# A layer of two blocks on one core: six row slots for the down rows and ten for the up rows behind the first 160 gathers, instead of sixteen for both

## The chip, the cores and the metric

The kernel runs on one core of a Trainium2 chip. Its time is the device time of one execution, in microseconds; lower is better. The engines are TensorE (PE; PEld is its weight load), VectorE (DVE), ScalarE (ACT), GpSimd (POOL) and SyncE (SP). Each has a queue of its own that it works off in order; they wait for each other on semaphores. DMAs are issued by SP and by POOL and run beside the engines.

## The reference, cut to what matters

Two hybrid layers follow each other on 512 tokens of width 1024, in float32. The change lies in the last part of the second one, a retrieval of experts: each token picks 16 of 16384 experts for each of 8 heads, and takes a row of 1024 numbers from two tables for each of them.

```python
        experts = jnp.take_along_axis(cand_i, pos, axis=-1)
        gates = jax.nn.softmax(top_s, axis=-1)
        u = expert_down[experts]
        vv = expert_up[experts]
        act = jax.nn.gelu(jnp.einsum("thkd,td->thk", u, hb, preferred_element_type=jnp.float32),
                          approximate=False)
        return jnp.einsum("thk,thkd->td", (gates * act).astype(vv.dtype), vv)
```

## The kernel before

The expert stage is `expert_stage` (line 3106). Its work is cut into 32 units: one of four tiles of 128 tokens and one of eight heads each. A unit has 16 expert rows per token. Units 0 to 15 (`u < WIDE`) are the first half of the tokens; beside them all engines but POOL also run the second half's projection, attention, delta rule, output and queries ("late stages"), woven in at fixed ticks. Units 16 to 31 have nothing beside them.

POOL issues the rows as indirect DMAs (line 3246), in the order of the list `order`:

- in the first half a row of the down table and a row of the up table are two gathers of 0.5 MB (128 tokens, 4 KB each). The list begins with the 16 down gathers of unit 0; then, quad by quad (four rows), it has four down gathers of unit u+1 and four up gathers of unit u. Unit 15 has no down gathers beside it, but the first three gathers of unit 16 before its third quad. There are 512 such gathers, the single ones;
- in the second half one gather fetches both rows, 1 MB. There are 256.

Below, "down 8.6" is the down gather of unit 8, row 6; "up 7.1" is the quad 1 of the up rows of unit 7; "both 16.3" is a double gather.

Who uses them: DVE multiplies a down row by its token and adds up (`dot`, line 3328, 1.22 us), which frees the row's place at once. A unit's 8 dots go through `weigh` on DVE and `coefs` on ACT to coefficients; then PE adds four up rows (16 matmuls, line 3515), which frees the four places together. By the ticks at line 3503 the sum of up u.g stands beside the dots of unit u+1, behind row 4g+2 or so: the up rows of a quad are used about a quad later than the down rows that stand beside them in `order`.

Where the rows land: there are 16 single slots (seats): 0 to 3 in `second_arena`, 4 to 7 in ring 1, 8 to 11 in ring 2, 12 to 15 in ring 0. The first 16 gathers turn over eight of them, the next 144 over twelve (seats 8 to 11 and 0 to 7), since ring 0 still holds weights of the late projection until `late_in.used`. What is left, 352 gathers, turns over all sixteen, down and up rows alike:

```python
        every = list(range(12, 16)) + some[0]
        single = [few[0][n % 8] for n in range(few[1])]
        single += [some[0][n % 12] for n in range(some[1] - few[1])]
        single += [every[n % GR] for n in range(2 * RK * WIDE - some[1])]
```

The double gathers turn over eleven places (`cells`): three of their own, then the pairs of seats 12 and 13, 14 and 15, 0 and 1, 2 and 3, and so on up to 10 and 11. Before POOL issues a gather it waits for what used the place last (lines 3224 and 3226): a dot (`dotted`) for a down row, the sum of the quad (`summed`) for an up row. While it waits, everything behind it in `order` waits too.

Of the kernel before, what the change touches and what calls it, by code (L numbers as in the profile page):

```python
# [37 lines left out]
RH, RK, NKEY = 8, 16, 128  # L38
# [3067 lines left out]
def expert_stage(k, t, halves, late, query_chunks, late_in, late_ring):  # L3106
# [6 lines left out]
    GR = 16  # L3113
    DR = 16
    QUADS = RK // 4
    WIDE = HT * RH
    with ExitStack() as ctx:
# [59 lines left out]
        order = [("down", 0, s) for s in range(RK)]  # L3177
# [8 lines left out]
        order += [("both", u, s) for u in range(WIDE, N) for s in range(RK) if u > WIDE or s >= 3]  # L3186
        place = {job: n for n, job in enumerate(order)}
        few, some = [list(range(8)), 16], [list(range(8, 12)) + list(range(8)), 160]
        every = list(range(12, 16)) + some[0]
        single = [few[0][n % 8] for n in range(few[1])]  # L3190
        single += [some[0][n % 12] for n in range(some[1] - few[1])]
        single += [every[n % GR] for n in range(2 * RK * WIDE - some[1])]
        cells = [None] * 3 + [(c, c + 1) for c in [12, 14, 0, 2, 4, 6, 8, 10]]
        last_in, taken, turn, before, seat, landing = {}, {}, [], [], [], []
        singles = doubles = 0
# [341 lines left out]
def second_block(k):  # L3537
    nc = k.nc
    with ExitStack() as ctx:
# [92 lines left out]
        lead = max(0, beat(HT * RH - 2, 4) - sum(stage.ticks for stage in late))  # L3632
        late.append(repeated_rows_stage(k, t, second, ctx, lead))
        expert_stage(k, t, t.halves, late, query_chunks, late_in, ring)


# [113 lines left out]
```

How the kernel before makes its waits and increments, by code:

```python
def post(eng, ins, sig):  # L103
    ins.then_inc(sig.sem, 1)
    sig.n += 1
    eng.wait_ge(sig.sem, sig.n)
# [56 lines left out]
    def stream(self, sp, last, ahead=SLOTS):  # L164
        upto = min(len(self.chunks), last + ahead)
        for g in range(self.issued, upto):
            if g >= SLOTS:
                sp.wait_ge(self.used.sem, g - SLOTS + 1)
            n = self.chunks[g][4]
            sp.dma_start(self.ring[g % SLOTS][:, :, 0:n], self.chunks[g][3]).then_inc(self.loaded[g % SLOTS], 16)
        self.issued = max(self.issued, upto)
# [1 line left out]
    def take(self, pe, g):  # L175
        pe.wait_ge(self.loaded[g % SLOTS], 16 * (g // SLOTS + 1))
        return self.ring[g % SLOTS]
# [25 lines left out]
    def multiply(self, pe, n):  # L204
        which, _, g = self.steps[n]
        w = self.k.take(pe, g)
        if n > 1:
            pe.wait_ge(self.row_in, n - 1 if n < self.alone else n)
        for kk in range(KD):
            strip = 32 * (kk % 4)
            last = pe.matmul(self.row_bank(n)[strip:strip + 32, :],
                             self.silu_c[:, which, kk:kk + 1].broadcast_to([P, 32]), w[:, kk, :],
                             start=(kk < 4), stop=(kk >= 4))
        last.then_inc(self.k.used.sem, 1)
        self.k.used.n += 1
# [1 line left out]
    def turn(self, pe, n):  # L218
        pe.wait_ge(self.row_in, n + 1)
        if n > 0:
            pe.wait_ge(self.columns_in, n)
# [5 lines left out]
    def copy_row(self, act, n):  # L228
        act.wait_ge(self.k.used.sem, self.steps[n][2] + 1)
        if n > 1:
            act.wait_ge(self.turned, n - 1)
```

## Time and profile before

| | |
|---|---|
| median of 3 runs | 2910.37 us (2905.1 to 2914.68) |
| the profiled execution | 2916.51 us, of it a span of 2914.7 us |
| busy in the span | PE 72%, DVE 58%, ACT 34%, POOL 32% |
| granted TensorE clock, mean | 0.824 |
| gathers of the stage | 768, issued from 1394.8 to 2888.3 us, 536.92 MB |

The span is the profiled time from the first to the last instruction; what lies around it is 1.8 us. The expert stage fills its second half: single gathers up to 2246 us, double ones from 2233 us to the end. Shares over the whole span say little here, since the stages have different limits; the section on rows has the stage in stretches.

### The profile page before, as it was taken

To read this page: it belongs to the slowest core of one execution; us is meant where nothing else is said; L and a number is where in the kernel's file an instruction comes from. 1 tells how busy PE (TensorE), PEld (TensorE's weight loads), DVE (VectorE), ACT (ScalarE), POOL (GpSimd) and SP (SyncE) were. 2 spreads that over 40 slices of the span, in tenths; PEclk is the share of its full clock that TensorE was granted. 3 is DMA by queue.
4 is the path that set the end of the run, shared out by engine and by line. 5 is a ranking of instruction groups with operands and counts; after the bars stand their busy time and mean duration, and the time that the engine had idled before them with its cause. 6 is when DMAs were issued, how large, how long until landed. Compare 5 with 4: busy or idle time off the path is not lost. (4 is left out here: it accounts for less than half of the span.)

```text
span 2914.7 us, 29054 instructions
## 1 busy us (share of the span) xinstructions
PE 2110.2 (72%) x9386; PEld 1214.3 (42%) x9386; DVE 1689.7 (58%) x3717; ACT 991.0 (34%) x2766; POOL 933.8 (32%) x835
## 2 busy tenths in 40 slices
PE   7999899999979899997997867759443333333333
PEld 3444444445558478776844435526220000000000
DVE  2058814345533332442677888875664877787775
ACT  2022402248740233122445643544544222222220
POOL 0000000013310000000366665776777444444442
PEclk8999999999989999988998768879666665565555
DMA  7114112222245443113699988999999999999997
GB/s 315 67 67 173 58 40 107 73 73 73 66 169 231 170 173 116 58 37 126 231 371 394 329 331 273 378 410 410 345 353 376 420 421 421 421 411 419 415 408 321
DMA packets 155207, 732.24 MB, mean 251 GB/s; under 512 B 17664, under 2 KB 43664, under 8 KB 110000
## 3 DMA queue, kind: packets, MB, share of 16 engines
q0 software_dynamic: 110592, 536.92, 46.9%
q1 hardware_dynamic: 44176, 192.57, 17.5%
q8 instruction: 75, 1.23, 0.2%
q10 hardware_dynamic: 288, 0.90, 0.1%
q14 instruction: 76, 0.62, 0.1%
HBM read 722.92 MB, written 7.42 MB: 251 GB/s over the span
## 5 line engine op out<-in xcount | busy, mean ns | idle before, releaser
L3515 PE MATMUL bank<-ring,xT 128*32 128x512 f32 x1464 | 389.6, 917 | 392.6 <-DVE xT L3351 225.1
L3328 DVE CUSTOM_DVE_ANT_0 ring<-ring,second_arena 128x1024 f32<-128x1024 f32 x278 | 340.9, 1226 | 141.4 <-DMA ring<-in_peer_experts,experts_stacked 70.7
L495 PE MATMUL bank<-hT,ring 128*128 128x512 f32 (+2 forms) x1168 | 398.2, 502 | 6.4 <-PEq L3650 1.8
L3515 PE MATMUL bank<-second_arena,xT 128*32 128x512 f32 x584 | 226.1, 972 | 204.5 <-DVE xT L3351 194.5
L3328 DVE CUSTOM_DVE_ANT_0 second_arena<-second_arena 128x1024 f32<-128x1024 f32 x234 | 287.6, 1229 | 116.6 <-DMA second_arena<-in_peer_experts,experts_stacked 53.0
L3515 PEld LDWEIGHTS bank<-ring,xT 128*32 128x32 f32 x1464 | 71.1, 144 | 581.3 <-issue 580.5
L3246 POOL DMA_INDIRECT ring<-in_peer_expert_up,experts_stacked x228 | 270.4, 1186 | 95.3 <-issue 64.9
L495 PEld LDWEIGHTS bank<-hT,ring 128*128 128x128 f32 (+1 forms) x1168 | 221.3, 190 | 187.4 <-issue 170.8
L3246 POOL DMA_INDIRECT second_arena<-in_peer_expert_down,experts x116 | 126.9, 1094 | 475.2 <-DVE experts L3305 421.1
L1416 POOL TENSOR_TENSOR xs_skip<-xs_rows,rows 128x512 f32<-128x512 f32 x16 | 24.7, 1545 | 707.8 <-ACT xs_rows L1294 618.7
L493 PE MATMUL bank<-ring,hT 128*128 128x512 f32 (+1 forms) x512 | 215.8, 582 | 5.5 <-DMA ring<-in_weights 4.6
L3246 POOL DMA_INDIRECT ring<-in_peer_experts,experts_stacked x138 | 151.9, 1100 | 197.1 <-PE bank L3515 157.2
L3246 POOL DMA_INDIRECT ring<-in_peer_expert_down,experts x140 | 151.8, 1085 | 108.6 <-issue 37.2
L3246 POOL DMA_INDIRECT second_arena<-in_peer_experts,experts_stacked x118 | 125.1, 1060 | 171.9 <-PE bank L3515 144.5
L3515 PEld LDWEIGHTS bank<-second_arena,xT 128*32 128x32 f32 x584 | 38.5, 150 | 298.5 <-issue 298.5
L3450 ACT ACTIVATE xT<-expert_coefs 32x2 f32<-32x2 f32 x512 | 103.9, 203 | 163.3 <-DVE expert_coefs L3366 116.1
L3490 ACT ACTIVATE expert_dots<-expert_dots 128x4 f32<-128x4 f32 x64 | 13.1, 205 | 417.2 <-DVE expert_dots L3328 417.1
L493 PEld LDWEIGHTS bank<-ring,hT 128*128 128x128 f32 x512 | 97.7, 192 | 120.9 <-issue 110.8
L1102 DVE SCALAR_TENSOR_TENSOR xbcT<-bank,cols,xbcT 128x511 f32<-128x511 f32 (+2 forms) x72 | 53.9, 749 | 102.5 <-ACT xbcT L1064 100.7
L1204 PE MATMUL bank<-ring,hT 128*128 128x512 f32 x240 | 108.0, 603 | 3.3 <-ACT silu_z_rows L1283 3.3
L3426 ACT ACTIVATE experts_stacked<-experts 32x4 int32<-32x4 int32 x512 | 105.8, 207 | 6.6
L1896 PE MATMUL bank<-second_arena,ring 128*128 128x256 f32 x384 | 92.5, 393 | 2.5 <-issue 2.5
(535 smaller groups left out, 3699.4 us busy)
## 6 DMA issues: line engine op xcount, KB each, us to landing
ring<-in_weights SPq DMA_DIRECT2D x66, 2048.0 KB, 7.9
ring<-in_weights SPq DMA_DIRECT2D x14, 1024.0 KB, 8.0
second_arena<-in_weights SPq DMA_DIRECT2D x12, 1024.0 KB, 8.2
decay<-acum_scratch SPq DMA_DIRECT2D x16, 512.0 KB, 5.2
ring<-in_peer_expert_up,experts_stacked POOLq DMA_INDIRECT x228, 6.7
ring<-in_peer_expert_down,experts POOLq DMA_INDIRECT x140, 6.4
ring<-in_peer_experts,experts_stacked POOLq DMA_INDIRECT x138, 14.9
x_rows<-in_x SPq DMA_DIRECT2D x1, 2048.0 KB, 12.3
```

Of the source, the lines that this page charges most:

```text
L493: last = pe.matmul(held[i][:, 0:n], fixed[:, which * ring.depth + kk, i * P:(i + 1) * P], w[:, kk, 0:n], **flags)
L495: last = pe.matmul(held[i][0:wide, 0:self.width], w[:, kk, i * P:i * P + wide], fixed[:, which * ring.depth + kk, :], **flags)
L1102: ins = dve.scalar_tensor_tensor(t.xbcT[:, j, back:T], bank[:, 0:T - back], k.col("conv_w", (3 - back) * 24 + j), t.xbcT[:, j, back:T], AL ...
L1204: last = pe.matmul(k.bank[7][:], k.hT[:, kk, c * P:(c + 1) * P], w[:, kk, :], start=(kk == 0), stop=(kk == KD - 1))
L1416: pool.tensor_tensor(skip[:], x3, bc(k.row("d_skip")[:, hs], 2, tall), ALU.mult)
L1896: last = pe.matmul(k.bank[6 + b][:, (i % 2) * H2:(i % 2 + 1) * H2], w[:, kk, i * P:(i + 1) * P], fixed[:, which * KD + kk, :], start=(whic ...
L3246: pool.indirect_dma_start(out=space(n), out_offset=None, in_=table, in_offset=bass.IndirectOffsetOnAxis(ap=rows, axis=0),).then_inc(here[l ...
L3328: post(dve, dve.tensor_tensor_reduce(row, row, tokens, 1.0, 0.0, ALU.mult, ALU.add, dots[:, u % 2, at:at + 1]), dotted)
L3426: ins = act.activation(mine, experts[blocks(q), i, h * RK + 4 * x:h * RK + 4 * x + 4], ACT.Copy)
L3450: ins = act.activation(mine, coef[blocks(q), u % 2, 4 * x + 2 * n:4 * x + 2 * n + 2], ACT.Copy)
L3490: post(act, act.activation(mine, mine, ACT.Gelu), gelued)
L3515: last = pe.matmul(sums[i][half][blocks(q), :], diag[(u * RK + 4 * g + q) % DR], rows[q][:, half * 512:(half + 1) * 512], start=(h == 0 an ...
```

## The change

The first 160 single gathers keep their seats. Behind them the down rows turn over six seats of their own (8 to 11, 0 and 1) and the up rows over ten (12 to 15 and 2 to 7). The order of the gathers, the double gathers' places, the work and the bytes stay the same.

```diff
         few, some = [list(range(8)), 16], [list(range(8, 12)) + list(range(8)), 160]
-        every = list(range(12, 16)) + some[0]
+        down_seats, up_seats = some[0][0:6], list(range(12, 16)) + some[0][6:12]
         single = [few[0][n % 8] for n in range(few[1])]
         single += [some[0][n % 12] for n in range(some[1] - few[1])]
-        single += [every[n % GR] for n in range(2 * RK * WIDE - some[1])]
+        downs = ups = 0
+        for kind, _, _ in [job for job in order if job[0] != "both"][some[1]:]:
+            if kind == "down":
+                single.append(down_seats[downs % 6])
+                downs += 1
+            else:
+                single.append(up_seats[ups % 10])
+                ups += 1
```

What a gather waits for follows from the seats. Before, each single gather waits for the user of the gather 16 places ahead of it in the list. Now a down gather waits for the dot six down rows back (before, mostly eight), and of the four up gathers of quad g the first two wait for the sum three quads back and the last two for the sum two quads back (before, all four two quads back).

POOL's queue where the change begins, gathers 160 to 179 of the list, down and up rows in turn, as it was. The semaphores go by names of earlier stages: here `decays_made` counts the dots and `unit_root` the sums, `mod2_sums_ready` is `late_in.used`, `dt_acum_rows` is `late_ring.used`, and `unit_routed` and `unit_products` say that a unit's experts are known and stacked.

```order
L3246 DMA ring0<-in_peer_expert_down_2,experts 128x1024 [waits mod2_sums_ready] x4
L3246 DMA ring2<-in_peer_expert_up_2,experts_stacked 128x1024 [waits unit_root] x4
L3246 DMA second_arena<-in_peer_expert_down_2,experts 128x1024 [waits decays_made] x4
L3246 DMA ring1<-in_peer_expert_up_2,experts_stacked 128x1024 [waits unit_root] x4
L3246 DMA ring0<-in_peer_expert_down_2,experts 128x1024 [waits decays_made,unit_routed]
L3246 DMA ring0<-in_peer_expert_down_2,experts 128x1024 [waits decays_made] x3
```

And now:

```order
L3253 DMA ring2<-in_peer_expert_down_2,experts 128x1024 [waits unit_root] x4
L3253 DMA ring0<-in_peer_expert_up_2,experts_stacked 128x1024 [waits mod2_sums_ready] x4
L3253 DMA second_arena<-in_peer_expert_down_2,experts 128x1024 [waits decays_made] x2
L3253 DMA ring2<-in_peer_expert_down_2,experts 128x1024 [waits decays_made] x2
L3253 DMA second_arena<-in_peer_expert_up_2,experts_stacked 128x1024 [waits decays_made] x2
L3253 DMA ring1<-in_peer_expert_up_2,experts_stacked 128x1024 [waits unit_root] x2
L3253 DMA ring2<-in_peer_expert_down_2,experts 128x1024 [waits decays_made,unit_routed]
L3253 DMA ring2<-in_peer_expert_down_2,experts 128x1024 [waits decays_made]
L3253 DMA second_arena<-in_peer_expert_down_2,experts 128x1024 [waits decays_made] x2
```

The first down gathers now take ring 2 and wait for sums; the up gathers take the fresh ring 0. From then on a quad's rows no longer share one wait: its down gathers lie in two groups of two, and so do its up gathers.

POOL's queue where the double gathers begin, from the first up gathers of unit 15 on, as it was:

```order
L3246 DMA ring0<-in_peer_expert_up_2,experts_stacked 128x1024 [waits unit_products,decays_made]
L3246 DMA ring0<-in_peer_expert_up_2,experts_stacked 128x1024 [waits decays_made] x3
L3246 DMA ring2<-in_peer_expert_up_2,experts_stacked 128x1024 [waits unit_root] x4
L3246 DMA second_arena<-in_peer_experts_2,experts_stacked 128x2048 [waits unit_products,dt_acum_rows]
L3246 DMA second_arena<-in_peer_experts_2,experts_stacked 128x2048 [waits dt_acum_rows] x2
L3246 DMA second_arena<-in_peer_expert_up_2,experts_stacked 128x1024 [waits decays_made] x4
L3246 DMA ring1<-in_peer_expert_up_2,experts_stacked 128x1024 [waits unit_root] x4
L3246 DMA ring0<-in_peer_experts_2,experts_stacked 128x2048 [waits unit_root] x2
L3246 DMA second_arena<-in_peer_experts_2,experts_stacked 128x2048 [waits unit_root] x2
L3246 DMA ring1<-in_peer_experts_2,experts_stacked 128x2048 [waits unit_root] x2
```

And now, over the same stretch:

```order
L3253 DMA ring1<-in_peer_expert_up_2,experts_stacked 128x1024 [waits unit_products,unit_root]
L3253 DMA ring1<-in_peer_expert_up_2,experts_stacked 128x1024 [waits unit_root]
L3253 DMA ring0<-in_peer_expert_up_2,experts_stacked 128x1024 [waits unit_root] x4
L3253 DMA second_arena<-in_peer_expert_up_2,experts_stacked 128x1024 [waits unit_root] x2
L3253 DMA second_arena<-in_peer_experts_2,experts_stacked 128x2048 [waits unit_products,dt_acum_rows]
L3253 DMA second_arena<-in_peer_experts_2,experts_stacked 128x2048 [waits dt_acum_rows] x2
L3253 DMA ring1<-in_peer_expert_up_2,experts_stacked 128x1024 [waits unit_root] x4
L3253 DMA ring0<-in_peer_expert_up_2,experts_stacked 128x1024 [waits unit_root] x4
L3253 DMA ring0<-in_peer_experts_2,experts_stacked 128x2048 [waits unit_root] x2
L3253 DMA second_arena<-in_peer_experts_2,experts_stacked 128x2048 [waits decays_made]
L3253 DMA second_arena<-in_peer_experts_2,experts_stacked 128x2048 [waits unit_root]
```

The last four up gathers (up 15.3) used to land in ring 1 and now land in ring 0. The fourth and fifth double gathers (both 16.3 and 16.4) take ring 0 in either kernel: they used to wait for the sum of up 15.0 and now wait for the sum of up 15.3, the last one of the half. The gathers behind them find places that dots or earlier sums have freed.

## Rows read from the trace of the kernel before

**Rows 1.** The page, part 2: DMA share in tenths and GB/s of 40 slices.

```profile
DMA  7114112222245443113699988999999999999997
GB/s 315 67 67 173 58 40 107 73 73 73 66 169 231 170 173 116 58 37 126 231 371 394 329 331 273 378 410 410 345 353 376 420 421 421 421 411 419 415 408 321
```

**Rows 2.** Windows: length, busy us (instructions) by engine, PE clock, DMA share, GB/s.

```profile
1690.00:1850.00 160.00, 109.78 (x674) 77.92 (x676) 132.87 (x266) 67.66 (x220) 101.68 (x93) 0.78 0.85 303
1850.00:2045.00 195.00, 144.48 (x731) 98.88 (x723) 140.10 (x318) 95.56 (x337) 139.66 (x125) 0.87 1.02 408
2045.00:2230.00 185.00, 75.66 (x847) 34.46 (x851) 117.31 (x277) 87.07 (x321) 147.09 (x124) 0.67 0.95 349
2230.00:2260.00 30.00, 13.42 (x72) 2.49 (x64) 6.65 (x17) 9.85 (x42) 17.58 (x19) 0.64 1.02 415
2260.00:2880.00 620.00, 218.59 (x976) 41.81 (x976) 473.83 (x1141) 148.60 (x568) 265.12 (x246) 0.58 1.01 417
```

**Rows 3.** Groups on POOL, 1686 to 2247 us: busy, mean ns, idle before.

```profile
L3246 POOL DMA_INDIRECT ring<-in_peer_expert_up,experts_stacked x180 | 216.2, 1201 | 77.9 <-issue 51.2 <-PE bank L3515 26.6
L3246 POOL DMA_INDIRECT second_arena<-in_peer_expert_down,experts x84 | 92.1, 1097 | 40.1 <-issue 22.6 <-DVE expert_dots L3328 17.5
L3246 POOL DMA_INDIRECT ring<-in_peer_expert_down,experts x84 | 89.9, 1071 | 36.4 <-issue 24.1 <-DVE expert_dots L3328 12.3
```

**Rows 4.** Timeline of POOL at 1712 us: start, length, instruction, idle before.

```profile
1712.15 0.94 POOL L3246 DMA_INDIRECT ring<-in_peer_expert_down,experts  x1 [0.30 <-issue]
1720.71 0.94 POOL L3246 DMA_INDIRECT ring<-in_peer_expert_up,experts_stacked  x1 [7.62 <-PE bank L3515]
```

**Rows 5.** Timeline of DVE at 1719 us, the dot of down 5.13.

```profile
1718.79 1.22 DVE L3328 CUSTOM_DVE_ANT_0 second_arena<-second_arena 128x1024 f32<-128x1024 f32 x1
```

**Rows 6.** Timeline of POOL at 1845 us.

```profile
1844.33 1.69 POOL L3246 DMA_INDIRECT second_arena<-in_peer_expert_down,experts  x1 [0.30 <-issue]
1846.32 0.94 POOL L3246 DMA_INDIRECT ring<-in_peer_expert_up,experts_stacked  x1 [0.30 <-issue]
```

**Rows 7.** Timeline of DVE at 1848 us, the dot of down 8.1.

```profile
1847.99 1.22 DVE L3328 CUSTOM_DVE_ANT_0 ring<-ring,second_arena 128x1024 f32<-128x1024 f32 x1
```

**Rows 8.** Timeline of SP's DMA queue at 1850 us.

```profile
1850.75 2.36 SPq L1659 DMA_DIRECT2D second_arena<-in_weights  x3
```

**Rows 9.** Timeline of POOL at 2030 us.

```profile
2030.07 0.94 POOL L3246 DMA_INDIRECT ring<-in_peer_expert_down,experts  x1 [0.30 <-issue]
2035.06 1.77 POOL L3246 DMA_INDIRECT ring<-in_peer_expert_up,experts_stacked  x1 [4.05 <-PE bank L3515]
```

**Rows 10.** Timeline of DVE at 2034 us, the dot of down 11.13.

```profile
2033.53 1.22 DVE L3328 CUSTOM_DVE_ANT_0 second_arena<-second_arena 128x1024 f32<-128x1024 f32 x1
```

**Rows 11.** Timeline of POOL, 2230 to 2260 us.

```profile
2230.53 0.94 POOL L3246 DMA_INDIRECT ring<-in_peer_expert_up,experts_stacked  x1 [0.30 <-issue]
...
2247.30 1.32 POOL L3246 DMA_INDIRECT ring<-in_peer_experts,experts_stacked  x1 [0.30 <-issue]
...
2259.59 1.69 POOL L3246 DMA_INDIRECT ring<-in_peer_experts,experts_stacked  x1 [1.45 <-PE bank L3515]
```

**Rows 12.** Timeline of PE, the sums of up 14.3 and up 15.3.

```profile
2228.00 3.33 PE L3515 MATMUL bank<-ring,xT 128*32 128x512 f32 x16 [7.48 <-DMA ring<-in_peer_expert_up,experts_stacked]
...
2256.87 1.92 PE L3515 MATMUL bank<-ring,xT 128*32 128x512 f32 x16 [1.71 <-DMA ring<-in_peer_expert_up,experts_stacked]
```

**Rows 13.** Timeline of DVE, the dot of both 16.3.

```profile
2259.24 1.22 DVE L3328 CUSTOM_DVE_ANT_0 ring<-ring,second_arena 128x1024 f32<-128x1024 f32 x1 [10.69 <-DMA ring<-in_peer_experts,experts_stacked]
```

**Rows 14.** Line 3246 alone, the one gather issued at 1720.71 us: issue to landing.

```profile
DMA to landing us min/median/max: 4.1/4.1/4.1
```

**Rows 15.** Line 3246 alone, gathers, 1865 to 2030 us: issue to landing.

```profile
DMA to landing us min/median/max: 12.0/15.9/20.8
```

**Rows 16.** Line 3246 alone, gathers, 2045 to 2230 us: issue to landing.

```profile
DMA to landing us min/median/max: 5.2/6.2/7.7
```

**Rows 17.** Line 3246 alone, gathers, 2260 to 2880 us: issue to landing.

```profile
DMA to landing us min/median/max: 9.5/14.9/20.2
```

## The prediction

> **What bounds the kernel now.** I read the page's slices first: from slice 20 on the DMA engines are nearly always busy, with two different rates, 330 to 410 GB/s and then about 420 [rows 1]. The windows cut this into stretches [rows 2]. (a) 1690 to 1850 us: DVE is busy 132.87 of 160 us with its own and the late stages' work, the DMA share is only 0.85; the program on DVE and PE sets the pace and the gathers run ahead of it. (b) 1850 to 2045: DMA share 1.02 at 408 GB/s, full; SP's weights for the late stages come on top of the gathers from 1850.75 on [rows 8], and a gather takes 15.9 us to land at the median [rows 15]. (c) 2045 to 2230: 124 gathers in 185 us, 1.49 each. POOL is busy 147.09 us, 1.19 a gather, and 0.30 between two is its own gap; that is the whole stretch. Landing takes 6.2 us [rows 16], so nothing piles up: POOL's issuing is the bound, and what it is late at 2045 stays. (d) 2260 to 2880: share 1.01 at 417 GB/s; 246 double gathers of 1.05 MB are 258 MB, which take 618 of the 620 us. Full again, with 14.9 us to land [rows 17]. So the end of the kernel is the start of (d) plus bytes by rate, and any moment in which the DMA engines stand idle in (b) or (d), or POOL in (c), is paid one for one.
>
> Then I read what POOL waits for with its single gathers, 1686 to 2247 us: 26.6 us for sums, 17.5 + 12.3 = 29.8 us for dots, all else is its own gap [rows 3]. That is what other seats can change.
>
> **The seats in the first half.** The list has four down, four up in turn, so POOL cannot pass a waiting down gather. Six down rows back instead of eight means that POOL stands at most six down rows, about twelve places, ahead of DVE, where it stood up to sixteen ahead. The ten up seats give little back: the last two of every four up gathers still wait for the sum two quads back, as all did before. Only the first two wait for less. So the old wait stays and a nearer one is added in front of it.
>
> Place one, at 1712 us. Down 6.3 was issued at 1712.15, and the next gather, up 5.0, waited 7.62 us for a sum and went at 1720.71 [rows 4]. Now down 6.3 waits for the dot of down 5.13, which ends at 1718.79 + 1.22 = 1720.01 [rows 5]; it goes at 1720.3 and the up gather behind it at 1721.6. The wait has changed its name and is 0.9 us longer. In stretch (a) this costs nothing at once: POOL is idle there for a third of the time and the rows land well before their use, under the cover of DVE's work.
>
> Place two, where that cover ends. Down 8.7 was issued at 1844.33, the four gathers of up 7.1 from 1846.32 on [rows 6]. Now down 8.7 needs the dot of down 8.1, ended at 1847.99 + 1.22 = 1849.21 [rows 7]. It goes at 1849.5, up 7.1 at 1850.8 to 1851.5. At 1850.75, when the weights fill the DMA engines [rows 8], four gathers fewer are done or in the queue. Four times 0.524 MB at 408 GB/s is 5.1 us of DMA time that was spent in the idle part of (a) and must now be spent in (b), where there is none left. Bounds: 0, if what DVE and PE wait for in (b) is each other and the late landings hide behind it; 6, which I get when I walk the lag from place to place through 1745 to 1850 us. I take **5**, since a share of 1.02 leaves no room.
>
> Place three, the end of (b). Down 12.3 went at 2030.07; up 11.0 waited 4.05 us for a sum and went at 2035.06 [rows 9]. Now down 12.3 needs the dot of down 11.13, ended at 2033.53 + 1.22 = 2034.75 [rows 10]; it goes at 2035.06, and up 11.0 one issue (0.94 + 0.30) later. POOL enters (c) **1.2** us later, bounds 0.9 (as at place one) and 1.7 (a long issue of 1.4 us and the gap). In (c) nothing is added: six down rows and their six up rows come round in 12 x 1.49 = 17.9 us, and a down row needs 6.2 to land, 1.2 for its dot and at most four issues, 6.0, in which POOL is at up rows: 13.4. Nothing is won back there either.
>
> **Into the double gathers.** Up 15.6, the third row of its quad, now waits for the sum of up 14.3, ended at 2228.00 + 3.33 = 2231.33 [rows 12], where it went at 2230.53 [rows 11]: 1.1 us, of which the queue may hide all. I take **1**.
>
> The large term is both 16.3. It went at 2247.30 behind the last up gather [rows 11], and waited for the sum of up 15.0, long done. It now waits for the sum of up 15.3, which starts at 2256.87 because its last row has only then landed [rows 12]. At that moment every gather issued has landed: the DMA queue is empty, and POOL may not issue. What such a gather can start at is in the trace: both 16.7, which had this very wait, went at 2259.59 [rows 11]. Queued behind it on POOL are all other double gathers, free or not. Its landing in before was just ahead of its dot at 2259.24 [rows 13]. How long a double gather takes to land into a quiet queue no row shows. From below: a single one took 4.1 us [rows 14], and a double one has another 0.524 MB, 1.25 us at (d)'s rate: 5.4, landing at 2265.0, 5.8 us late. From above: 6.2 us, the median where POOL issues without a pause [rows 16], plus 1.25: 7.45, landing at 2267.0, 7.8 us late. I take **7**, nearer the upper end, since the gathers behind it come 1.24 us and more apart as in (c), and the stream as a whole starts with that delay.
>
> The Trainium skill, DMA: Bandwidth & Descriptors, section on the anatomy of one DMA on the gpsimd path, fits a DMA to about 2.0 us plus bytes over 436 GB/s. For 1 MiB this estimate is 4.4 us, which would make this term 4.8 and the sum below 12; for 0.5 MiB it gives 3.2 where the row has 4.1, so the trace does not quite agree.
>
> Afterwards POOL issues at least one gather per 2 us and the engines need 2.5 for each, so they stay full and nothing is made up. Both 16.11 waits for the sum of both 16.0 in either kernel, and eight gathers, 20 us of transfer, are queued ahead of it.
>
> Sum: 5 + 1.2 + 1 + 7 = **14 us** later. The profiled execution took 2916.5 us, so it becomes 2930.7; it lies 6.1 us over the median of the runs. The same 14 us on the median 2910.4 gives **2924 us**, 0.5% more.
>
> **Rivals.** About 0.3%, 8.7 us, is what a measurement of this kernel can tell from no change.
>
> 1. Slower as summed, by 9 to 20 us (2919 to 2930): chance 0.50.
> 2. The lag of the first half is hidden: the late stages' own chain on PE and DVE sets the pace in (b), not the landings. For it: DVE is busy 140 of 195 us there, PE 144. Against: the share of 1.02. Then the terms are 0 + 1.2 + 0 to 1 + 5.8 to 7 = 7 to 9, 2917 to 2919, just within 0.3%. Chance 0.27.
> 3. In (b) six down seats are too few. A down row that takes 15.9 us to land, with 1.2 for the dot and 1.5 for the issue, comes round in 18.6 us; six of them and their up rows need only 12 x 1.29 = 15.5 us of DMA time. If the landing does not shorten, each round loses 3.1 us, and about nine rounds 28 us: with the other terms up to 2947. For most of it landing does shorten, since it is queueing, but at 4 or 6 us of it lost I reach 2928 to 2935 and more. It decides where DVE's own pauses in (b) outlast the shorter queue. Chance 0.15.
> 4. Faster: the sums held POOL up, and ten up seats free it. If all 26.6 us of waits on sums went and none on dots took their place, POOL would be further ahead at 1850 us and the idle 15% of (a), 24 us, would carry more of the bytes: 26.6 less the 8 of the switch to double gathers is 18.6 us, 2892. It needs the dots to be ahead of POOL at each place where the sums hold it; at places one and three they end only 0.7 and 0.3 us before the gather that waited for the sum went, so the wait is only passed on. Chance 0.06.
> 5. That the change does nothing: the order of the queue shows that it moves both kinds of waits, so only hidden costs could make it so; 0.02.
>
> **How the numbers follow.** The likeliest is 1, at 2924. The range must take in 2, whose lower end with the quiet landing at its shortest and 3 to 4 us of spread between the runs' medians is 2912, and the lower part of 3, up to 2936. Faster by over 0.3%: 0.05. Within 0.3%: most of 2, the edge of 1 and 5, 0.30. Slower: 0.65.
>
> **What the profile after would show.** Between 1686 and 2247 us POOL's waits for sums shrink to a few us and those for dots grow from 29.8 to 50 or more. Place two: the up gathers of unit 7, quad 1, come after the weights. Window 2045 to 2230 looks the same, 5 to 7 us later; a lag of 1 us there means rival 2, of 10 or more rival 3. Both 16.3 is issued right behind the sum of up 15.3, after 8 to 11 us of idle POOL, and DVE waits about 17 us for it instead of 10.69; a dip of the DMA share under 1 around 2265 to 2275 us. The rest runs at 417 GB/s. The prediction is wrong if the first double gathers start no later against the last sum than before, if POOL's lag at 2045 is nothing or negative, or if the double gathers gain anything on their way to the end.

## The result, and the profile after

| | before | after |
|---|---|---|
| median of 7 runs | 2912.92 us (2905.10 to 2921.26) | 2925.80 us (2924.33 to 2937.67) |
| the profiled execution | 2916.51 us, span 2914.7 | 2937.67 us, span 2935.9 |
| busy in the span | PE 72%, DVE 58%, ACT 34%, POOL 32% | PE 72%, DVE 58%, ACT 34%, POOL 31% |

The time after is 1.0055 times the time before (95%: 1.0036 to 1.0073), 12.9 us between the medians. That ratio is taken over all the runs and is 16 us of 2913; the medians alone make 1.0044. The change makes the kernel slower by half a per cent.

The profiled execution of after is the slowest of its seven, 21 us longer than the one of before. Not all of that is the change's: gather 160, the first one with a new seat, went at 1685.99 us in before and at 1693.94 us in after, and up to there the two kernels are the same. So a lag is counted from gather 160 below, by which 8.0 us have to come off. The kernel before on POOL, at gathers 160 and 256, at one of its waits for sums near the end of (b) (the other is in [rows 9]) and at gather 376 (timeline: start, length, instruction, idle before):

```profile
1685.99 1.88 POOL L3246 DMA_INDIRECT ring<-in_peer_expert_down,experts  x1 [0.30 <-issue]
...
1851.58 1.31 POOL L3246 DMA_INDIRECT ring<-in_peer_expert_down,experts  x1 [0.31 <-issue]
...
2020.65 0.96 POOL L3246 DMA_INDIRECT ring<-in_peer_expert_up,experts_stacked  x1 [6.27 <-PE bank L3515]
...
2041.34 1.69 POOL L3246 DMA_INDIRECT second_arena<-in_peer_expert_down,experts  x1 [0.30 <-issue]
```

The kernel after on POOL, same view. In order: gather 160; down 6.0, 6.2 and 6.3 and up 5.0 (place one); down 8.7 and up 7.1 (place two); gather 256; down 12.3 and up 11.0 (place three); gather 376; up 15.6; the last up gather; both 16.3 and 16.4.

```profile
1693.94 1.88 POOL L3253 DMA_INDIRECT ring<-in_peer_expert_down,experts  x1 [0.30 <-issue]
...
1717.68 0.94 POOL L3253 DMA_INDIRECT ring<-in_peer_expert_down,experts  x1 [2.22 <-DVE expert_dots L3335]
...
1725.69 0.94 POOL L3253 DMA_INDIRECT second_arena<-in_peer_expert_down,experts  x1 [4.81 <-DVE expert_dots L3335]
1728.93 0.94 POOL L3253 DMA_INDIRECT second_arena<-in_peer_expert_down,experts  x1 [2.31 <-DVE expert_dots L3335]
1730.17 0.94 POOL L3253 DMA_INDIRECT ring<-in_peer_expert_up,experts_stacked  x1 [0.30 <-issue]
...
1860.15 0.94 POOL L3253 DMA_INDIRECT second_arena<-in_peer_expert_down,experts  x1 [0.30 <-issue]
1861.39 1.31 POOL L3253 DMA_INDIRECT second_arena<-in_peer_expert_up,experts_stacked  x1 [0.30 <-issue]
...
1867.48 0.94 POOL L3253 DMA_INDIRECT ring<-in_peer_expert_down,experts  x1 [0.30 <-issue]
...
2049.99 1.80 POOL L3253 DMA_INDIRECT second_arena<-in_peer_expert_down,experts  x1 [0.86 <-DVE expert_dots L3335]
2052.10 0.96 POOL L3253 DMA_INDIRECT second_arena<-in_peer_expert_up,experts_stacked  x1 [0.30 <-issue]
...
2057.09 1.74 POOL L3253 DMA_INDIRECT ring<-in_peer_expert_down,experts  x1 [0.31 <-issue]
...
2246.86 0.94 POOL L3253 DMA_INDIRECT second_arena<-in_peer_expert_up,experts_stacked  x1 [1.96 <-PE bank L3522]
...
2261.88 0.94 POOL L3253 DMA_INDIRECT ring<-in_peer_expert_up,experts_stacked  x1 [0.30 <-issue]
2274.90 0.94 POOL L3253 DMA_INDIRECT ring<-in_peer_experts,experts_stacked  x1 [12.09 <-PE bank L3522]
2276.14 0.94 POOL L3253 DMA_INDIRECT ring<-in_peer_experts,experts_stacked  x1 [0.30 <-issue]
```

Gather 256 is 15.9 us later than in before, a lag of 8.0 us (15.90 less 7.95); gather 376 has 7.8. The last four columns of the table in the next section go on with that: the sum of up 15.3 has 7.4, the dot of both 16.3 has 13.3, the end 13.2. The loss is made at two places, one in front of gather 256 and one between the last sum of the first half and the first double rows.

PE and DVE of the kernel after where the double gathers begin, same view: the sum of up 15.3 (the one of [rows 12]) and the dot of both 16.3 (of [rows 13]).

```profile
2272.18 1.92 PE L3522 MATMUL bank<-ring,xT 128*32 128x512 f32 x16 [1.42 <-DMA ring<-in_peer_expert_up,experts_stacked]
```

```profile
2280.47 1.22 DVE L3335 CUSTOM_DVE_ANT_0 ring<-ring,second_arena 128x1024 f32<-128x1024 f32 x1 [16.61 <-DMA ring<-in_peer_experts,experts_stacked]
```

DVE waits 16.61 us for that row, where it was 10.69 [rows 13]. The windows of the kernel after (columns as in [rows 2]); the last three are within the wait and just behind it:

```profile
1690.00:1850.00 160.00, 104.33 (x621) 73.69 (x618) 131.74 (x265) 71.58 (x237) 92.11 (x88) 0.78 0.82 287
1850.00:2045.00 195.00, 139.14 (x722) 93.30 (x721) 138.94 (x314) 88.13 (x307) 133.36 (x124) 0.86 1.01 399
2045.00:2230.00 185.00, 87.00 (x901) 44.62 (x899) 121.85 (x289) 88.02 (x316) 146.53 (x123) 0.69 0.97 357
2285.00:2880.00 595.00, 208.77 (x944) 40.10 (x936) 460.19 (x1112) 146.71 (x564) 255.02 (x233) 0.60 1.01 418
...
2265.00:2270.00 5.00, 2.87 (x16) 0.68 (x16) 0.00 (x0) 4.83 (x18) 0.00 (x0) 0.50 1.02 410
2270.00:2275.00 5.00, 2.69 (x20) 0.50 (x16) 0.00 (x0) 1.23 (x6) 0.10 (x1) 0.89 0.10 40
2275.00:2280.00 5.00, 0.00 (x0) 0.00 (x0) 0.00 (x0) 0.00 (x0) 3.78 (x5) 0.80 0.66 229
```

Before had 303 GB/s in (a) and 417 in (d) [rows 2]. After has 287 in (a), the same 418 behind 2285 us, and a hole in front of it: between 2270 and 2275 us the DMA engines move 40 GB/s. Groups on POOL in the kernel after, 1686 to 2265 us (as [rows 3]):

```profile
L3253 POOL DMA_INDIRECT ring<-in_peer_expert_up,experts_stacked x152 | 171.8, 1130 | 46.4 <-issue 45.1 <-PE bank L3522 1.2
L3253 POOL DMA_INDIRECT ring<-in_peer_expert_down,experts x112 | 120.9, 1080 | 79.2 <-DVE expert_dots L3335 52.1 <-issue 27.1
L3253 POOL DMA_INDIRECT second_arena<-in_peer_expert_down,experts x58 | 62.5, 1077 | 39.0 <-DVE expert_dots L3335 24.7 <-issue 14.3
L3253 POOL DMA_INDIRECT second_arena<-in_peer_expert_up,experts_stacked x36 | 41.9, 1163 | 12.7 <-issue 10.5 <-PE bank L3522 2.3
```

POOL's waits for sums went from 26.6 us to 1.2 + 2.3 = 3.5; its waits for dots from 29.8 to 52.1 + 24.7 = 76.8. In all it stands 24 us longer in such waits, but it isn't 24 us late: the 352 gathers from 160 on were busy for 12 us less in all (390 instead of 402), and a wait takes the place of the gap of 0.30, so that the last of them has a lag of 7.9 us.

What DVE saw of the first half's loss: the dots of down 8.0 and down 9.0, in the kernel before and then in the kernel after, and in after the weights for the late stages on SP's queue ([rows 8] before).

```profile
1843.98 1.22 DVE L3328 CUSTOM_DVE_ANT_0 ring<-ring,second_arena 128x1024 f32<-128x1024 f32 x1
1890.60 1.23 DVE L3328 CUSTOM_DVE_ANT_0 ring<-ring,second_arena 128x1024 f32<-128x1024 f32 x1 [4.43 <-issue]
```

```profile
1854.03 1.23 DVE L3335 CUSTOM_DVE_ANT_0 second_arena<-second_arena 128x1024 f32<-128x1024 f32 x1
1904.37 1.23 DVE L3335 CUSTOM_DVE_ANT_0 ring<-ring,second_arena 128x1024 f32<-128x1024 f32 x1 [1.58 <-issue]
```

```profile
1860.57 1.59 SPq L1659 DMA_DIRECT2D second_arena<-in_weights  x3
```

Up to the end of (a) POOL is late and DVE hardly is: the dot of down 8.0 has a lag of 2.1 us, that of down 9.0 one of 5.8. Over all profiles of the next section this is clearer. In the six with six down seats in (a) the dot of down 8.0 comes on average 1.2 us earlier than in the five with sixteen, and the dot of down 9.0 comes 4.0 us later.

Issue to landing of the kernel after, line 3253 alone: the gather at 2274.90; those from 1866 to 2032 us; those from 2060 to 2245 us.

```profile
DMA to landing us min/median/max: 5.4/5.4/5.4
DMA to landing us min/median/max: 6.2/11.8/16.2
DMA to landing us min/median/max: 5.3/6.4/9.0
```

### The profile page after: what moved, and what is told of

Read it like the earlier page. It is cut to its first block and busy times, and to the rows that moved or that the text cites. A ratio compares the mean times of both kernels' runs of the same rounds, so it can differ in the third digit from the quotient of the medians.

```text
span 2935.9 us, 29054 instructions
## 1 busy us (share of the span) xinstructions
PE 2105.1 (72%) x9386; PEld 1210.9 (41%) x9386; DVE 1690.4 (58%) x3717; ACT 990.7 (34%) x2766; POOL 921.9 (31%) x835
## 5 line engine op out<-in xcount | busy, mean ns | idle before, releaser
L3335 DVE CUSTOM_DVE_ANT_0 ring<-ring,second_arena 128x1024 f32<-128x1024 f32 x306 | 375.6, 1227 | 161.0 <-DMA ring<-in_peer_experts,experts_stacked 76.9
L3522 PE MATMUL bank<-second_arena,xT 128*32 128x512 f32 x712 | 271.8, 946 | 237.8 <-DVE xT L3358 201.3
L3335 DVE CUSTOM_DVE_ANT_0 second_arena<-second_arena 128x1024 f32<-128x1024 f32 x206 | 252.9, 1228 | 108.7 <-DMA second_arena<-in_peer_experts,experts_stacked 52.1
L3522 PEld LDWEIGHTS bank<-ring,xT 128*32 128x32 f32 x1336 | 70.1, 144 | 558.2 <-issue 557.6
L3253 POOL DMA_INDIRECT ring<-in_peer_expert_up,experts_stacked x196 | 223.3, 1139 | 62.3 <-issue 57.7
L3253 POOL DMA_INDIRECT second_arena<-in_peer_expert_down,experts x88 | 93.7, 1064 | 473.6 <-DVE experts L3312 421.2
L3253 POOL DMA_INDIRECT ring<-in_peer_expert_down,experts x168 | 181.4, 1080 | 155.0 <-DVE expert_dots L3335 69.0
L3522 PEld LDWEIGHTS bank<-second_arena,xT 128*32 128x32 f32 x712 | 46.9, 147 | 342.3 <-issue 342.2
L3497 ACT ACTIVATE expert_dots<-expert_dots 128x4 f32<-128x4 f32 x64 | 13.2, 205 | 417.4 <-DVE expert_dots L3335 417.2
```

Source lines behind the costliest of these rows:

```text
L3253: pool.indirect_dma_start(out=space(n), out_offset=None, in_=table, in_offset=bass.IndirectOffsetOnAxis(ap=rows, axis=0),).then_inc(here[l ...
L3335: post(dve, dve.tensor_tensor_reduce(row, row, tokens, 1.0, 0.0, ALU.mult, ALU.add, dots[:, u % 2, at:at + 1]), dotted)
L3497: post(act, act.activation(mine, mine, ACT.Gelu), gelued)
L3522: last = pe.matmul(sums[i][half][blocks(q), :], diag[(u * RK + 4 * g + q) % DR], rows[q][:, half * 512:(half + 1) * 512], start=(h == 0 an ...
```

## The experiments

Every further kernel was timed in five rounds beside the kernel before, six to twelve executions of each and 23 to 35 of before. "Places" are the pairs of seats that the double gathers turn over; their order stands in two lists, lines 3123 and 3193, always changed alike, and the diffs show the second. The lags come from the profiled executions, counted from gather 160 against the profile of before, in us: at gathers 256 and 376 (POOL), at the sum of up 15.3 (PE), at the dot of both 16.3 (DVE), at the end. "16 shared" means all sixteen seats in turn, as in before.

| kernel | seats behind gather 160 | median (before beside it) | ratio (95%) | 256 | 376 | sum 15.3 | both 16.3 | end |
|---|---|---|---|---|---|---|---|---|
| after | 6 + 10 | 2925.80 (2912.92) | 1.0055 (1.0036 to 1.0073) | 8.0 | 7.8 | 7.4 | 13.3 | 13.2 |
| last places first | 16 shared | 2916.15 (2911.98) | 1.0013 (1.0000 to 1.0025) | 2.1 | 2.6 | -1.9 | 3.9 | 3.7 |
| six, free places first | 6 + 10 | 2921.36 (2911.98) | 1.0030 (1.0012 to 1.0048) | 5.7 | 7.9 | 5.0 | 5.0 | 4.1 |
| sixteen, free places first | 16 shared | 2910.67 (2911.98) | 0.9992 (0.9978 to 1.0005) | -0.2 | -1.3 | -2.4 | -2.4 | -2.5 |
| six and eight | 6 + 8 | 2927.00 (2911.98) | 1.0052 (1.0033 to 1.0072) | 8.4 | 10.8 | 11.4 | 13.9 | 14.8 |
| early | 6 + 10 to 255, then 16 | 2917.51 (2910.21) | 1.0025 (1.0005 to 1.0045) | 5.9 | -0.9 | -2.0 | -2.0 | -1.6 |
| middle | 6 + 10 in 256 to 399 | 2913.48 (2910.21) | 1.0009 (0.9997 to 1.0022) | 2.3 | 2.7 | -0.1 | -0.1 | 0.2 |
| late | 6 + 10 from 400 | 2912.48 (2910.21) | 1.0007 (0.9993 to 1.0021) | 2.0 | 1.1 | 2.1 | 2.1 | 2.1 |
| seven and nine | 7 + 9 | 2917.16 (2910.21) | 1.0021 (1.0007 to 1.0036) | 5.7 | 2.0 | 3.0 | 3.0 | 3.4 |
| early and middle | 6 + 10 to 399, then 16 | 2921.14 (2910.49) | 1.0032 (1.0017 to 1.0048) | 6.3 | 4.9 | 4.1 | 4.1 | 4.9 |
| early, again | as early | 2917.51 (2910.49) | 1.0019 (1.0004 to 1.0034) | 6.1 | -0.7 | -2.9 | -2.9 | -2.5 |
| five and eleven | 5 + 11 | 2929.23 (2910.49) | 1.0061 (1.0041 to 1.0081) | 12.2 | 17.0 | 13.8 | 13.8 | 13.4 |

How far a single profile can be trusted is in the table too: the kernels that have sixteen shared seats up to gather 256 or 400 differ from before by -0.2 to 2.3 at gather 256, and those that measured within 0.1% end at -2.5 to 2.1. Two us of lag are nothing. Means say more: at gather 256 the six profiles with six down seats up to there have 6.7 us, the four with sixteen and before itself 1.2.

### Last places first: the switch alone

The seats stay as before; only the first double gathers behind the last up gathers are sent to the pairs 4 and 5, 6 and 7, which hold the quad of up 15.3.

```diff
-        cells = [None] * 3 + [(c, c + 1) for c in [12, 14, 0, 2, 4, 6, 8, 10]]
+        cells = [None] * 3 + [(c, c + 1) for c in [4, 6, 12, 14, 0, 2, 8, 10]]
```

> Seats of the first half as before; only the double gathers' places are in another order (pairs from seats 4, 6, 12, 14, 0, 2, 8, 10), so that both 16.3 and 16.4 wait for the sum of up 15.3, as in the changed kernel. Theory (an empty DMA queue at the switch costs about 6 us by itself, the first half the rest): 6 us slower than before, 5 to 7, ratio about 1.002, the whole lag between the last up row's landing and both 16.3's, and the same pace up to there. Rival (the switch costs nothing, since the second half makes it up): no change. Rival (the switch is all of the loss): 13 to 16 us slower.

Measured: 1.0013 (1.0000 to 1.0025), 4.2 us between the medians. POOL of this kernel at the last up gather and the first two double ones, then DVE at the dot of both 16.3, then the windows around:

```profile
2240.05 0.93 POOL L3246 DMA_INDIRECT ring<-in_peer_expert_up,experts_stacked  x1 [0.30 <-issue]
2253.35 0.94 POOL L3246 DMA_INDIRECT ring<-in_peer_experts,experts_stacked  x1 [12.36 <-PE bank L3515]
```

```profile
2258.85 1.23 DVE L3328 CUSTOM_DVE_ANT_0 ring<-ring,second_arena 128x1024 f32<-128x1024 f32 x1 [16.51 <-DMA ring<-in_peer_experts,experts_stacked]
```

```profile
2250.00:2255.00 5.00, 1.92 (x16) 0.50 (x16) 0.00 (x0) 0.00 (x0) 1.35 (x2) 1.00 0.03 5
```

These are the waits of after to within 0.3 us (12.09 and 16.61) with the seats of before, and the hole, 5 GB/s for 5 us. The lag grows by 3.9 + 1.9 = 5.8 us from the sum of up 15.3 to the dot. The profile shows the switch as a cause of its own, about 6 us. The times alone are weaker: at the bottom of the interval it would be nothing, at the top 7.3 us.

### Six, free places first: the seats of after without the switch

The seats of after; the double gathers begin with the pairs 8 and 9, 10 and 11, which down rows have left long before, and take ring 0 last.

```diff
-        cells = [None] * 3 + [(c, c + 1) for c in [12, 14, 0, 2, 4, 6, 8, 10]]
+        cells = [None] * 3 + [(c, c + 1) for c in [8, 10, 0, 2, 4, 6, 12, 14]]
```

> Six and ten seats as in the changed kernel, but the double gathers take the places that are free first (pairs from seats 8, 10, 0, 2, 4, 6, 12, 14). Theory: the 6 us at the switch are gone, the lag of the first half stays: 7 to 9 us slower than before, ratio about 1.0027, with POOL 8 us late at the 376th gather and the same lag at the end. Rival (only the switch costs, the lag of the first half is hidden): no change, within 2 us. Rival (the first half costs all of it): 13 us slower still.

Measured: 1.0030 (1.0012 to 1.0048), 9.4 us between the medians. POOL at the last up gather and at both 16.3, and DVE at its dot:

```profile
2245.50 0.94 POOL L3253 DMA_INDIRECT ring<-in_peer_expert_up,experts_stacked  x1 [0.30 <-issue]
2246.74 0.95 POOL L3253 DMA_INDIRECT ring<-in_peer_experts,experts_stacked  x1 [0.30 <-issue]
```

```profile
2258.36 1.23 DVE L3335 CUSTOM_DVE_ANT_0 ring<-ring,second_arena 128x1024 f32<-128x1024 f32 x1 [10.74 <-DMA ring<-in_peer_experts,experts_stacked]
```

The wait of 12.09 us is gone, DVE waits 10.74 us as in before, and from the sum to the dot the lag doesn't grow (5.0 and 5.0). What is left, 0.30%, is the first half's part. With the switch's 0.13% that makes 0.43%, against 0.55% measured for both (0.44% between the medians), which the intervals allow. The expected lag of 8 us was there at gather 376 (7.9) and not at the end (4.1), although the medians are 9.4 us apart; the section on the prediction comes back to that.

### Sixteen, free places first: does the order of places help by itself?

```diff
-        cells = [None] * 3 + [(c, c + 1) for c in [12, 14, 0, 2, 4, 6, 8, 10]]
+        cells = [None] * 3 + [(c, c + 1) for c in [12, 14, 8, 10, 0, 2, 4, 6]]
```

> Sixteen shared seats as before, and the double gathers take the places that are free first (pairs from seats 12, 14, 8, 10, 0, 2, 4, 6). Theory: the DMA queue was never empty at the switch, POOL's idle 6.10 us before both 16.5 were covered by 8 queued gathers: no change, within 1 us. Rival (the switch of before cost something too): 1 to 5 us faster.

Measured: 0.9992 (0.9978 to 1.0005), no change that can be told. So the kernel above loses by its seats and not by its places; nor is there anything to win at the switch of before.

### Six and eight: are the ten up seats worth anything?

Two up seats are left empty, the places are those of after.

```diff
+        down_seats, up_seats = some[0][0:6], list(range(12, 16)) + some[0][6:10]
...
+                single.append(up_seats[ups % 8])
```

> Six down seats and only eight up seats behind the first 160 gathers; two seats stay empty until the double gathers. Double gathers' places as in the changed kernel. Theory (the two additional up seats give little back, since POOL stands behind the down rows): within 3 us of the changed kernel, 13 to 17 us slower than before. Rival (the ten up seats gain something that the six down seats lose): clearly slower than the changed kernel, 20 us or more over before, with waits for sums of 20 us and more back on POOL.

Measured: 1.0052 (1.0033 to 1.0072), the time of after. It was expected within 3 us of after, and waits for sums of 20 us and more, the rival's sign, didn't come back (7.8 us). The profile suggests that the equal times hide two differences that cancel. POOL at both 16.3:

```profile
2269.23 0.94 POOL L3253 DMA_INDIRECT ring<-in_peer_experts,experts_stacked  x1 [7.63 <-PE bank L3522]
```

With eight up seats the last quad lands in seats 2 to 5, so this gather waits for the sum of up 15.2 and not for the last one: 7.63 us, and the lag grows by 2.5 us there (11.4 to 13.9) instead of 5.9. Before that it is 4 us larger than in after (11.4 against 7.4). So the ninth and tenth up seat may give back some 4 us of the first half, and not the nothing that equal times suggest; the evidence is one profile each, with a spread of 2 us and more. They don't give back what the down rows lose.

### Early, middle, late: where in the first half?

Each has six and ten seats in one stretch of the list and all sixteen in turn elsewhere. Where the mode changes, the places are taken in the order of their last use, so that the change of mode brings no wait of its own; the double gathers' places are free ones. Early has the stretch 160 to 255:

```diff
-        single += [every[n % GR] for n in range(2 * RK * WIDE - some[1])]
+        for upto, narrow in [(256, True), (512, False)]:
+            last_use = {s: n for n, s in enumerate(single)}
+            oldest = sorted(range(GR), key=lambda s: (last_use.get(s, -1), s))
+            down_seats = oldest[0:4] + oldest[8:10]
+            up_seats = oldest[4:8] + oldest[10:16]
...
```

Middle has `[(256, False), (400, True), (512, False)]` in the place of that list, late `[(400, False), (512, True)]`, early and middle `[(400, True), (512, False)]`.

> Six down and ten up seats for single gathers 160 to 255 alone, the stretch in which the DMA engines still have idle time; from 256 on all sixteen in turn again, oldest first, and the double gathers take the places free first. Theory (the lookahead missing when the late stages' weights fill the queue is DMA time lost for good): POOL 5 us late at gather 256 and still 4 to 5 us late at gather 400 and at the end, 4 to 5 us slower than before. Rival (only waits inside the full stretch cost): late at 256, but level again by 400, no change at the end.

> Six and ten seats for single gathers 256 to 399 alone, the full stretch; before and behind it sixteen in turn, and the double gathers take the places free first. Theory: the rows queued at gather 256 are all there, the narrower lookahead costs only POOL's later start into the next stretch: 1 to 3 us late at 400 and at the end. Rival (six down seats are too few while a row takes 16 us to land): 6 to 8 us late at 400 and at the end, and none of the loss in the run with the early stretch alone.

> Six and ten seats from single gather 400 on alone, where POOL's own issuing sets the pace, and the double gathers take the places free first. Both theories: no change, within 1 us at the last up rows and at the end; over 2 us late there would mean that down rows are waited for in this stretch too.

Measured: early 1.0025 (1.0005 to 1.0045), middle 1.0009 (0.9997 to 1.0022), late 1.0007 (0.9993 to 1.0021). Late costs nothing that can be told, as (c) was read. Nor does middle by itself. Late ends 2.1 us late in its profile, just over the 2 us that were to mean waits for down rows in (c), but POOL waits for no dot behind gather 376, there or in any other of the profiles. Early makes the lag, 5.9 us at gather 256, but its profile has lost it again by gather 376, where 4 to 5 us were expected. Since that doesn't go with a time that is 7.3 us longer, it was run again, and beside it early and middle together:

> The kernel with six and ten seats for gathers 160 to 255 alone, once more. Its timed runs were 7 us slower than before at the median, but its profiled one had lost 6 us at gather 256 and won them back by gather 376. If winning back is what it does as a rule, the median is within 3 us of before and the profile shows the same; if the profiled one was an exception, the median is 4 to 7 us slower again and the profile more often keeps the lag.

> Six and ten seats for single gathers 160 to 399, both stretches at once, then sixteen in turn; the double gathers take the places free first. Theory now (the rows come 5 to 6 us late through the full stretch, and with six down seats POOL cannot leave it without them, since it waits for late dots; with sixteen it waits for sums that PE's late stages time anyway): the whole first-half lag of 6 to 8 us at gather 376 and at the end, though early and middle alone left 0 to 2 in their profiles. Rival (the losses of the two stretches simply add): 1 to 3 us.

Measured: early again 1.0019 (1.0004 to 1.0034), its profile again 6.1 us late at gather 256 and 0.7 us early at 376; early and middle 1.0032 (1.0017 to 1.0048), the whole of what six seats throughout cost, and 4.9 us of lag at 376 (6 to 8 were expected, 1 to 3 by its rival). What early does near the end of (b), on POOL, with its waits above the gap of 0.30:

```profile
2002.45 1.55 POOL L3259 DMA_INDIRECT ring<-in_peer_expert_up,experts_stacked  x1 [0.43 <-PE bank L3528]
2016.28 0.94 POOL L3259 DMA_INDIRECT second_arena<-in_peer_expert_up,experts_stacked  x1 [3.00 <-PE bank L3528]
2027.94 0.93 POOL L3259 DMA_INDIRECT ring<-in_peer_expert_up,experts_stacked  x1 [0.90 <-PE bank L3528]
```

And early and middle, at the same point of the program:

```profile
2018.83 0.94 POOL L3259 DMA_INDIRECT ring<-in_peer_expert_down,experts  x1 [1.08 <-DVE expert_dots L3341]
2021.05 1.00 POOL L3259 DMA_INDIRECT ring<-in_peer_expert_down,experts  x1 [1.28 <-DVE expert_dots L3341]
...
2032.50 0.94 POOL L3259 DMA_INDIRECT ring<-in_peer_expert_down,experts  x1 [2.52 <-DVE expert_dots L3341]
```

In before POOL stands 6.27 us (at 2020.65, above) and 4.05 us [rows 9] for sums there: it is early, and has to wait. With sixteen seats a POOL that comes 6 us late waits that much less and is back in its place. With six down seats it stands for dots instead, and the dots are late with the rows. The sums over gathers 256 to 375 agree: before stands 17.1 us for sums there, early 11.3 and 10.5 in its two profiles; early and middle stands 0.3 for sums and 27.1 for dots. So in the profiles the lag needs both stretches: the early one makes it, the middle one keeps it.

The times don't bear this out. By them the stretches simply add: early alone is 7.3 and 7.0 us slower between the medians, middle alone 3.3, and both together 10.7. For the second run of early either a median within 3 us of before or a kept lag had been expected; neither came. That slack wins the lag back is thus seen in two profiled executions of early and not shown for its runs at large.

### Seven and nine, five and eleven: the dose

Both with free places first.

```diff
+        down_seats, up_seats = some[0][0:7], list(range(12, 16)) + some[0][7:12]
...
-        cells = [None] * 3 + [(c, c + 1) for c in [12, 14, 0, 2, 4, 6, 8, 10]]
+        cells = [None] * 3 + [(c, c + 1) for c in [8, 10, 0, 2, 4, 6, 12, 14]]
```

> Seven down and nine up seats behind the first 160 gathers, the double gathers take the places free first. Theory (POOL's distance ahead of DVE in down rows sets the lag): one down seat more halves the lag or better, 2 to 4 us late at gather 376 against 8 with six, and 2 to 4 us slower than before. Rival (any split costs, because pooled seats even out what separate ones cannot): 7 to 9 us as with six. Rival (six was under a balance that seven meets): faster than before by up to 3 us.

```diff
+        down_seats, up_seats = some[0][0:5], list(range(12, 16)) + some[0][5:12]
...
-        cells = [None] * 3 + [(c, c + 1) for c in [12, 14, 0, 2, 4, 6, 8, 10]]
+        cells = [None] * 3 + [(c, c + 1) for c in [8, 10, 6, 12, 14, 0, 2, 4]]
```

> Five down and eleven up seats behind the first 160 gathers, the double gathers take the places free first. Theory (POOL's distance ahead of DVE in down rows): 9 to 10 us late at gather 256 against 6 to 8 with six, 12 to 18 us late at gather 376 and at the end, against 8 and 4 to 8 with six. Rival (the loss is the same for any split): 7 to 9 us. Waits for dots over 100 us, none for sums.

Measured: seven 1.0021 (1.0007 to 1.0036), five 1.0061 (1.0041 to 1.0081), where six measured 1.0030 and sixteen shared seats 0.9992; in all four both 16.3 goes right behind the last up gather. The intervals of five and seven lie apart, and those of six and seven lie above that of sixteen, so a split doesn't cost the same whatever it is. Between seven and six the times can't tell: seven is 7.0 us slower between the medians where 2 to 4 was expected, though its lag at gather 376 was the expected one, 2.0.

One sign failed. POOL's waits for dots, which should have passed 100 us with five, were 70.1 in its profile, against 58.9 with seven and 76.4 with six; those for sums were 1.9. The gathers themselves were busy for 402 us with five and 389 with six. So the dose shows in the lag and the time, not in the total of POOL's waits for dots, and no run says why its gathers took longer. Windows of (a) and (b) with five down seats:

```profile
1690.00:1850.00 160.00, 105.40 (x656) 74.60 (x648) 132.90 (x263) 67.68 (x220) 94.77 (x85) 0.79 0.80 279
1850.00:2045.00 195.00, 141.13 (x690) 92.82 (x691) 132.47 (x300) 89.78 (x320) 136.19 (x121) 0.84 1.01 398
```

Fewer down seats move fewer bytes in (a): 303 GB/s before, 287 in after, 279 with five. Five seats lose 12.2 us up to gather 256 and another 4.8 in (b), by one profile.

## Why the prediction was right

The forecast was 2924 us and 14 us; the measurement has 2925.8 and 12.9 between the medians (16 by the ratio over all the runs), the profile 13.2. By its own steps:

- **Place one** went as told: down 6.3 waits for dots where up 5.0 had waited for a sum, and up 5.0 went at 1730.17, which is 1.5 us later than before (0.9 was expected), at no cost at once.
- **Place two, 5 us (0 to 6)** was about right, though not by the wait it named. Up 7.1 was issued at 1861.39, behind the weights, which came at 1860.57, as told. But down 8.7 didn't wait for a dot at all ([0.30 <-issue]): POOL was already late by then from the places ahead, and up 7.1 is 7.1 us behind where 4.5 was expected. Gather 256 has a lag of 8.0 in after. The means of all profiles, 6.7 and 1.2, make it 5.5 us, so that most of the difference between 5 and 8 is the spread of single executions. By them the bytes agree too: (a) has 287 to 292 GB/s with six down seats and 298 to 305 with sixteen, a mean of 11 GB/s less over 160 us, 1.8 MB or three to four gathers (it is 285 to 289 against 299 to 303 where the window is laid from 4 us behind each profile's gather 160). And DVE becomes late only between down 8.0 and down 9.0, when the weights have come, as the mechanism asks.
- **"A share of 1.02 leaves no room"** isn't borne out as the reason for keeping that lag. In both profiles of early, with sixteen seats behind gather 256, a (b) of 411 and 406 GB/s takes it back (0.9 and 0.7 us early at 376). The room was in POOL's waits for sums, 10.3 us of them at the end of (b). That is near rival 2's world; six down seats close it, because POOL then waits for dots which are late themselves. The times of early, 7 us longer, don't show the winning back.
- **Place three, 1.2 us:** down 12.3 did wait for a dot, 0.86 us. But the lag at gather 376 is no larger than at 256 (7.8 and 8.0), so nothing was added on top. The two terms together, 6.2 us, measured 7.8 in this pair of profiles.
- **(c)** looks the same, 147 us of POOL and 6.4 us to land. Late, with six down seats in it alone, measured 1.0007, 2.3 us that can't be told from nothing; its lag grows by 1.0 us from gather 376 to the sum of up 15.3, where those of the kernels with sixteen seats there shrink by 0.8 to 4.5. But after, six with free places first, and five shrink too (0.4, 2.9 and 3.2), and POOL waits for no dot there. The term of nothing stands within what was measured. **Up 15.6** waited 1.96 us for its sum, and the queue hid it: the last up gather lags as much as gather 376 did, 7.9 us (2261.88, in before 2246.1). The term of 1 was 0.
- **The switch, 7 us (5.8 to 7.8)** measured 5.9 in after and 5.8 alone. The place, the wait and the sum that ends it were as told (POOL 12.09 us where 8 to 11 was expected, DVE 16.61 where 17 was). The size was taken too near the upper bound: a double gather into an empty queue landed in 5.4 us, which was the lower one.

The sum, 5 + 1.2 + 1 + 7, measured 7.8 - 0.4 + 5.9 = 13.3. The total is right partly by luck: the terms of the first half were set 1.6 us too small, the last two 2.5 us too large, and these cancel. Rival 3, too few down seats in (b), didn't come with six: landing did shorten, from 15.9 us [rows 15] to 11.8, so the rows came round in time. With five it may show, 4.8 us more in (b), though landing is shorter still (10.3 us). Rival 4 fell: the waits for sums went, as it said, and 47 us of waits for dots came in their place.

The Trainium skill, DMA: Bandwidth & Descriptors, section on the anatomy of one DMA on the gpsimd path, has a fit by which the estimate for 1 MiB is 4.4 us; the gather of that size landed in 5.4 us, so the measurement decides against it here, by the same 1 us as at 0.5 MiB (3.2 against 4.1 [rows 14]).

**What stays open.** Times and profiles don't agree on the first half. The early kernel's two profiles end 1.6 and 2.5 us ahead of before's, as far as the kernels that lose nothing, and its medians are 7.3 and 7.0 us longer. It isn't alone: between the medians six with free places first is 9.4 us slower and ends with a lag of 4.1, early and middle 10.7 and 4.9, seven 7.0 and 3.4, five 18.7 and 13.4, middle 3.3 and 0.2. The other five agree within 1.2 us, after among them. A lag is one execution against one of before, so either most executions lose more than the profiled ones did, or something that the profile doesn't show in these stretches costs them; no run told these apart. By the times the stretches add within their intervals: early 0.25 or 0.19%, middle 0.09%, late 0.07%, against 0.30% (0.12 to 0.48) for all three. The first half's total is therefore shown by times, and where in it the loss is made, kept or won back by profiles alone. No version beats before.

## What to carry to other kernels

When two streams share slots and one engine issues both in order, splitting the slots need not free the stream that gets more of them: here the issuer could only run ahead as far as the narrower one let it, and everything behind its next gather waited as well. Look at the place where the slots change hands. A first user that needs the last one released cost about the latency of a transfer here, 6 us by the profiles, with idle DMA engines beside it, and the order of a list of places decided it. And slack in an issuer, here 10 us of waits for sums, can take back a lag only as long as what it waits for is not itself late from that lag; two profiles show it, the times don't. So time a variant often before you believe what its one profile says of 5 us in 2900.

## What the runs showed of the hardware

A gather of 128 rows of 8 KB into an empty queue landed in 5.4 us, one of 128 rows of 4 KB in 4.1 us [rows 14]; the difference, 1.3 us, is 0.524 MB at about 400 GB/s, near the full stream's 418. By this, an estimate from these two landings, about 2.9 us of either are no transfer. The queue runs dry fast: POOL's last gather before the wait went at 2261.88 us, and the windows have 410 GB/s up to 2270 us and 40 in the 5 us behind it. And landing shortened with the seats while the rate hardly changed: in the full stretch (b) it was 15.9 us at 408 GB/s before, 11.8 us at 399 GB/s in after and 11.1 us at 407 GB/s in middle, which has six down seats in that stretch alone.
